# Router fed by token rows turned in the output projection, layer norm by statistics, small expert matmuls spread, last weights in pieces

## The chip, the cores and the metric

The kernel runs on one core of a Trainium2 chip. The core has a matrix engine (TensorE, PE in the profile; PEld is its weight load), a vector engine (VectorE, DVE), a scalar engine (ScalarE, ACT), GpSimd (POOL) and SyncE (SP), which issues most of the DMAs; ScalarE issues a few. Sixteen DMA engines move the data. The metric is the device time of one execution in microseconds. Three runs of the kernel before gave 2296.88, 2298.74 and 2298.82 us, median 2298.74.

## The reference, cut to what matters

Two blocks run one after the other on 256 tokens of width 1024. The change touches the second half of the second block: output projection, layer norm, router, a mixture of 32 experts (each token uses four), and a last layer norm.

```
x   = layer_norm(ALPHA * x + merged @ w_out, ln1_g, ln1_b)
logits = x @ router_w + router_b
top_val, top_idx = top_k(logits, 4);  gates = softmax(top_val)
for each expert e, on the tokens that chose it:
    gt = min(x @ w_gate[e] + b_gate[e], 7);  up = clip(x @ w_up[e] + b_up[e], -7, 7)
    y  = (gt * sigmoid(1.702 * gt) * (up + 1)) @ w_down[e] + b_down[e]
ffn = sum over the four experts of gate * y
out = layer_norm(ALPHA * x + ffn, ln2_g, ln2_b)
```

The weights w_gate, w_up and w_down are 32 x 1024 x 1024 each, in float32: 402.7 MB, all of which are read.

## The kernel before, in words

All activations of the first stages lie turned, with features on the 128 partitions: xT[:, d, 0:256] is block d (of eight) of the features, for 256 tokens. Each engine's program is one list in the order of the code; semaphores tie the lists together. The eight PSUM banks are handed out in turn by take(e, name); filled(name) is the semaphore value at which the bank has its result, emptied(name) the one at which it has been read.

Dense projections use weights in two halves. hi(t) is ScalarE's cast of weight tile t (four quarters of 128x1024), lo(t) is DVE's rest of it, and rows(...) issues the three matmuls for each of eight k. W_GATE are the gate projections, W_PA and W_PB (two tiles) the two branch projections, W_PB + 2 and W_PB + 3 the output projection w_out. The banks ("pa", d), ("pb", d) and ("wx", d) hold the results.

Behind the output projection stands the layer norm, on features that lie on partitions. TensorE adds over partitions with a matrix of 1/1024 (the mean, L810), ScalarE squares, TensorE adds again (L827), ScalarE takes the root, DVE the reciprocal, and DVE and ScalarE scale all eight blocks. TensorE multiplies with the router matrix rw (L835), turns the tokens back (L842), and turns the logits (L849). DVE finds the four largest and the positions of each token in its expert's list (the counting matmuls L854 to L856); ScalarE takes the exponentials; DVE makes G, the gate weights.

The experts are worked in 16 pairs b, with up to 64 tokens for each of the two. chosen(b) makes selection matrices Sx by comparison; gather(b) (L874) multiplies the token rows yN with them and so gathers and turns the tokens in one; XT holds the result. both(...) (L905) are the matmuls with expert weights: for each of eight k, the pair's two experts at the same time in the two halves of the columns. A pair is gate, up (each with a bias matmul, L931), the scatter of the pair before (L891, into the four banks accs), the gather of the pair after, the turn of the hidden values (L942), and down. ledger() behind pair 0 puts the expert's bias rows into accs (L963) and counts whether any expert has over 64 tokens; further pairs for such experts stand in If blocks.

The expert weights come through a ring of seven slots of 2048 KB, 12 loads for a pair, in the order gate, up, down. Load u goes into slot u % 7 and waits until TensorE has used load u - 7 (s_wused). Loads 0 to 6 take slots of the stages before as these come free.

At the end s_fin says that accs are whole. DVE adds ALPHA times the token rows, takes statistics (L1581, L1585, L1587), ScalarE the root, DVE scales and shifts (L1598, L1600), and SP stores.

## Time and profile before

| what | before |
|---|---|
| median of 3 runs | 2298.74 us |
| the profiled execution's own time | 2301.83 us |
| its span, first to last instruction | 2300.0 us |
| PE busy | 2104.4 us, 91% |
| DVE busy | 827.8 us, 36% |
| ACT busy | 575.4 us, 25% |
| DMA | 593.89 MB, mean 258 GB/s |
| mean granted TensorE clock | 0.968 |

Busy time is the time in which an engine has an instruction under way; a matmul's end is modelled, so a busy PE is not PE at its peak. The chain of waits goes back from the last instruction to what released it, and so on to the start. Its shares are PE 73%, DMA 15%, DVE 6%, ACT 3%. DMA is on the chain almost only as waiting for the experts' up weights (12% of the span).

### The profile page before, as it was taken

The numbers are of one execution on the slowest core, as the hardware profiler recorded it, in microseconds if no ns is written. First come the engines' busy times: TensorE is split into PE (matmuls) and PEld (weight loads), VectorE is DVE, ScalarE is ACT, GpSimd is POOL, SyncE is SP. The second block draws the span as 40 slices with busy tenths as digits, with TensorE's granted clock in tenths as the row PEclk, the third lists the DMA queues.
The fourth block names the chain that finished last, engine by engine and source line by source line (L and its number), as shares of the span: only waits on it lengthen the run. The fifth ranks groups of instructions, "written<-read, shape, count | busy, mean of one in ns | idle before, by whom it ended". The sixth has DMA issues, their size and how long they took to land.

```text
span 2300.0 us, 27009 instructions
## 1 busy us (share of the span) xinstructions
PE 2104.4 (91%) x11534; PEld 1402.2 (61%) x11534; DVE 827.8 (36%) x1453; ACT 575.4 (25%) x955; POOL 71.5 (3%) x119
## 2 busy tenths in 40 slices
PE   6988999999899889999998889998988999989886
PEld 3766888878687568999987843333333333333332
DVE  3353534352385656755465431111111111111113
ACT  3222423242242545544365220000000000000000
POOL 0000000000000320000041000000000000000000
PEclk7999999999999999999999989999999999999998
DMA  9543334233431564545524559999999999999994
GB/s 357 183 147 109 110 111 146 99 112 101 147 106 50 196 196 147 184 152 200 182 94 168 208 226 412 424 428 428 428 428 427 428 427 427 428 428 428 428 428 203
DMA packets 157228, 593.89 MB, mean 258 GB/s; under 512 B 6416, under 2 KB 79120, under 8 KB 132016
## 3 DMA queue, kind: packets, MB, share of 16 engines
q1 hardware_dynamic: 155104, 589.53, 64.8%
q10 hardware_dynamic: 2000, 2.57, 0.4%
q8 instruction: 94, 1.54, 0.3%
q14 instruction: 30, 0.25, 0.0%
HBM read 591.03 MB, written 1.05 MB: 257 GB/s over the span
## 4 chain that ended last, share of the span: by engine, by line
PE 73%; DMA 15%; DVE 6%; ACT 3%; issue 2%; SPq 1%; ACTq 0%; DVEq 0%
PE ps L905 21%; PE ps L278 13%; PE ps L279 13%; PE ps L280 13%; DMA ring<-in_w_up_dram 12%; PE ps L874 3%; DMA ring<-in_ada_w_dram 3%; PE ps L891 3%; DVE wr L1012 2%; PE ps L385 2%; DMA ring<-in_even_w_in_dram 1%; SPq L2044 1%; PE ps L399 1%; ACT wr L1614 1%; PE ps L942 1%
## 5 line engine op out<-in xcount | busy, mean ns | idle before, releaser
L905 PE MATMUL ps<-ring,big 128*64 128x512 f32 x3072 | 693.1, 607 | 81.9 <-DMA ring<-in_w_up_dram 51.3
L905 PEld LDWEIGHTS ps<-ring,big 128*64 128x64 f32 x3072 | 249.8, 140 | 496.3 <-issue 484.8
L278 PE MATMUL ps<-h_hi,wr 128*128 128x512 f32 (+1 forms) x960 | 342.9, 357 | 28.0 <-DVE h_lo L1064 24.9
L1012 DVE TENSOR_TENSOR wr<-ring,wr 128x1024 fp32r<-128x1024 f32 (+1 forms) x248 | 285.8, 1212 | 142.2 <-ACT wr L1614 142.1
L279 PE MATMUL ps<-h_lo,wr 128*128 128x512 f32 (+1 forms) x960 | 334.5, 348 | 0.0
L280 PE MATMUL ps<-h_hi,wr 128*128 128x512 f32 (+1 forms) x960 | 334.1, 348 | 0.0
L1614 ACT CAST wr<-ring 128x1024 fp32r<-128x1024 f32 (+1 forms) x248 | 238.7, 1032 | 128.0 <-PE ps L280 101.6
L278 PEld LDWEIGHTS ps<-h_hi,wr 128*128 128x128 f32 x960 | 186.0, 194 | 60.2 <-issue 34.5
L279 PEld LDWEIGHTS ps<-h_lo,wr 128*128 128x128 f32 x960 | 186.0, 194 | 23.8 <-issue 2.9
L280 PEld LDWEIGHTS ps<-h_hi,wr 128*128 128x128 f32 x960 | 185.6, 193 | 22.3
L1463 DVE TENSOR_SCALAR hT<-ps 128x512 f32<-128x512 f32 x32 | 20.6, 686 | 259.4 <-PE ps L931 259.4
L1476 DVE TENSOR_SCALAR hT<-ps 128x512 f32<-128x512 f32 x32 | 22.0, 688 | 239.5 <-PE ps L931 239.5
L278 PE MATMUL ps<-x_hi,wr 128*128 128x256 f32 x352 | 104.7, 297 | 1.8 <-DVE x_lo L1275 1.2
L1918 ACT COPY big<-ps 128x512 f32<-128x512 f32 x16 | 9.4, 586 | 370.9 <-PE ps L874 370.9
L279 PE MATMUL ps<-x_lo,wr 128*128 128x256 f32 x352 | 101.2, 287 | 0.0
L280 PE MATMUL ps<-x_hi,wr 128*128 128x256 f32 x352 | 101.1, 287 | 0.0
L1490 DVE COPY xT<-ps 128x512 f32<-128x512 f32 x16 | 11.1, 692 | 221.4 <-PE ps L905 221.4
L1930 ACT ACTIVATE hT<-hT 128x512 f32<-128x512 f32 x32 | 19.6, 630 | 261.2 <-DVE hT L1463 261.2
L278 PEld LDWEIGHTS ps<-x_hi,wr 128*128 128x128 f32 x352 | 69.1, 196 | 6.7 <-issue 4.4
L279 PEld LDWEIGHTS ps<-x_lo,wr 128*128 128x128 f32 x352 | 69.3, 197 | 0.2
L874 PEld LDWEIGHTS ps<-hT,big 128*128 128x128 f32 x512 | 62.3, 199 | 11.5 <-issue 11.5
L280 PEld LDWEIGHTS ps<-x_hi,wr 128*128 128x128 f32 x352 | 69.1, 196 | 0.0
(293 smaller groups left out, 2578.0 us busy)
## 6 DMA issues: line engine op xcount, KB each, us to landing
ring<-in_w_gate_dram SPq DMA_DIRECT2D x64, 2048.0 KB, 22.1
ring<-in_w_up_dram SPq DMA_DIRECT2D x64, 2048.0 KB, 19.7
ring<-in_w_down_dram SPq DMA_DIRECT2D x64, 2048.0 KB, 22.2
ring<-in_ada_w_dram SPq DMA_DIRECT2D x24, 2048.0 KB, 10.7
ring<-in_ffn_w_up_dram SPq DMA_DIRECT2D x44, 1024.0 KB, 7.6
ring<-in_ffn_w_down_dram SPq DMA_DIRECT2D x16, 1408.0 KB, 6.1
ring<-in_w_in_dram SPq DMA_DIRECT2D x9, 2048.0 KB, 8.2
ring<-in_odd_w_qkv_dram SPq DMA_DIRECT2D x6, 2048.0 KB, 8.1
```

The costliest lines, as they stand in the source:

```text
L278: e.matmul(o, l[0], r[0], start=first, stop=False)
L279: e.matmul(o, l[0], r[1], start=False, stop=False)
L280: return e.matmul(o, l[1], r[0], start=False, stop=last)
L385: ins = e.matmul(pt[32 * g:32 * g + 32, :], s2[:, 2 * g + h, :], wt[:, 2 * g + h, :], start=h == 0, stop=h == 1, skip_group_check=True)
L399: ins = e.matmul(bank(("sq", q))[:, 0:NT[q]], onesd[:, :], part[k % 2][:, 0:NT[q]], start=k == 0, stop=k == KC - 1, skip_group_check=True)
L874: ins = e.matmul(pt[:, P * c:P * c + P], yN[:, n, P * (4 * hf + c):P * (4 * hf + c) + P], Sx[turn_of(b)][:, 0, n, :], start=n == 0, stop=n ...
L891: ins = e.matmul(ps[2 * q + n][:, :], SgT[turn_of(b)][:, P * q:P * q + P], ySB[turn_of(b)][:, n, :], start=False, stop=False, skip_group_c ...
L905: ins = e.matmul(pts[hf][HALF[z], :], lhs[:, k, HALF[z]], wt[:, k % 4, 512 * hf:512 * hf + 512], start=k == 0, stop=False, skip_group_chec ...
L942: ins = e.transpose(pt[:, P * c:P * c + P], eighth(hid[:, 1, :], 4 * hf + c), ident)
L1012: e.tensor_tensor(wr[:, x], ring[:, x], h.bitcast(F32), SUB).then_inc(s_wlo, 1)
L1614: e.copy(wr[:, o], ring[:, SLOT * (t % 3) + 1024 * p:SLOT * (t % 3) + min(1024 * p + 1024, width[t])]).then_inc(s_whi, 1)
L2044: e.dma_start(view(ring, SLOT * MPLACE[m], KC, 512), a["ada_w"][m // 12].rearrange("(k p) n -> p k n", p=P)[:, :, 512 * (m % 12):512 * (m ...
```

## The change

It has five parts.

1. **Router and layer norm.** The gains and shifts of the first layer norm are no longer applied to the tokens. DVE multiplies the gain into the router matrix rw, and takes the sums that the mean and the shift need; one matmul, ("rs", 0), adds them over partitions. In the output projection, turn_rows(d) takes the place of the mean: for each block d, TensorE turns both halves of the tokens into the banks ("z", n, i), and multiplies the same blocks, as they are, with rw into ("lgt", n). DVE takes mean and variance from the z banks with bn_stats; ScalarE writes the normalised token rows yN. The gain and the shift are applied when XT is read out of PSUM, from g8b8, which 16 small DMAs on SP's queue load. DVE and ScalarE now also read XT out in four operations each.
2. **Order around it.** hi(W_PB) goes ahead of the sigmoids, the bias cast behind the last weights; lo(W_PB + 3) and the bias halves are made between the results of the output projection; the gate weights (weigh) are made behind the first four comparisons.
3. **Ledger spread.** ledger(b) does a part of the work behind each of the pairs 2, 4, 5, 6, 8, 10 and 12. In it the residual, ALPHA times yN times the gain, is also added to accs by matmuls with alphaI. The gain and the shift come as rows of 1024 words in one partition, by two DMAs on ScalarE's queue, word by word.
4. **Last weights.** The second half of up and all of down of the last pair are loaded in pieces (PIECES: load, first k, last k), with a semaphore for each; both() waits for each piece at its own k. In every pair, the second half of XT and HT is waited for at k = 4.
5. **Last norm.** last_scatter finishes tokens 0 to 127 first (s_fin 1), then the others. DVE takes statistics straight from accs, ScalarE normalises out of PSUM, DVE multiplies and adds.

```diff
+    LAST = 12 * (NE // 2 - 1)
+    PIECES = [(LAST + 6, 0, 2), (LAST + 6, 2, 3), (LAST + 6, 3, 4), (LAST + 8, 0, 2), (LAST + 8, 2, 4),
+              (LAST + 10, 0, 2), (LAST + 10, 2, 3), (LAST + 10, 3, 4)]
+    in_pieces = {u + z for u, _, _ in PIECES for z in range(2)}
...
+        pt = take(e, ("rs", 0))
+        e.wait_ge(s_rwsum, 1)
+        e.matmul(pt[:, 0:64], ones[:, :], sums, start=True, stop=True).then_inc(fullsem(("rs", 0)))
...
+        def turn_rows(d):
+            if d == 0:
+                for n in range(2):
+                    take(e, ("lgt", n), hold=True)
+            if d % 4 == 0:
+                for n in range(2):
+                    take(e, ("z", n, d // 4), hold=True)
             e.wait_ge(*emptied(("wx", d)))
+            if d == 0:
+                e.wait_ge(*emptied(("rs", 0)))
+            for n in range(2):
+                x = xT[:, d, P * n:P * n + P]
+                ins = e.transpose(bank(("z", n, d // 4))[:, P * (d % 4):P * (d % 4) + P], x, ident)
+                if d % 4 == 3:
+                    ins.then_inc(fullsem(("z", n, d // 4)))
+            for n in range(2):
+                x = xT[:, d, P * n:P * n + P]
+                ins = e.matmul(bank(("lgt", n))[:, 0:NE], x, rw[:, d, :], start=d == 0, stop=d == KC - 1,
+                               skip_group_check=True)
+                if d == KC - 1:
+                    ins.then_inc(fullsem(("lgt", n)))
...
-                    mean(d - 1)
+                    turn_rows(d - 1)
             wlast[W_PB + 2 + i] = filled(("wx", 4 * i + 3))
...
-        p2 = take(e, ("var", 0))
-        for k in range(KC):
-            e.wait_ge(s_sq, 4 * KC + k + 1)
-            e.matmul(p2[:, 0:L], onesd[:, :], part[k % 2][:, 0:L], start=k == 0,
-                     stop=k == KC - 1).then_inc(s_squsd if k < KC - 1 else fullsem(("var", 0)))
-
-
-        pt = take(e, ("lg", 0))
-        e.wait_ge(s_rw, 16)
-        for k in range(KC):
-            e.wait_ge(s_y, k + 1)
-            ins = e.matmul(pt[0:NE, 0:L], rw[:, k, :], xT[:, k, 0:L], start=k == 0, stop=k == KC - 1)
-        ins.then_inc(fullsem(("lg", 0)))
-
+        turn_rows(KC - 1)
+        for n in range(2):
...
+        def last_scatter(b):
+
+            for n in range(2):
+                e.wait_ge(*emptied(("y", b, n)))
+            for q in range(2):
+                for n in range(2):
                     ins = e.matmul(ps[2 * q + n][:, :], SgT[turn_of(b)][:, P * q:P * q + P], ySB[turn_of(b)][:, n, :], start=False,
                                    stop=False, skip_group_check=True)
-            ins.then_inc(s_scat)
-
-        def both(pts, lhs, u, first):
+                ins.then_inc(s_fin)
...
+        def both(pts, lhs, u, first, second):
 
             for k in range(KC):
+                if k == 4:
+                    e.wait_ge(*second)
                 v = u + 2 * (k // 4)
-                if k % 4 == 0:
+                if k % 4 == 0 and v not in in_pieces:
                     for z in range(2):
-                        e.wait_ge(s_w[(v + z) % 7], 16 * ((v + z) // 7 + 1))
+                        e.wait_ge(*landed_expert(v + z))
+                for i, (x, k0, _) in enumerate(PIECES):
+                    if (x, k0) == (v, k % 4):
+                        e.wait_ge(s_piece[i], 32)
...
                     e.wait_ge(*emptied(("xt", b, 0)))
-                    e.wait_ge(*emptied(("xt", b, 1)))
-                both(pts, XT[turn_of(b)], u + 4 * v, None)
+                both(pts, XT[turn_of(b)], u + 4 * v, None, emptied(("xt", b, 1)))
...
+        def ledger(b):
+
+            if b == 2:
+                pt = take(e, ("gT", 0), bank=7)
+                for n in range(2):
+                    ins = e.transpose(pt[0:NE, P * n:P * n + P], G[:, n, :], ident)
+                ins.then_inc(fullsem(("gT", 0)))
+            if b in (4, 8):
...
+            if b in (6, 10):
...
+            if b == 5:
+                e.wait_ge(*emptied(("gT", 0)))
...
+        gl, bl = (col(x, 0, 8).unsqueeze(2).to_broadcast([P, KC, NE]) for x in ("l1g", "l1b"))
+        rwb = view(part[0], 0, KC, NE)
+        e.wait_ge(s_rw, 16)
+        at = mark(e.tensor_tensor(rwb, rw, bl, MULT))
+        e.wait_ge(*at)
+        at = mark(e.tensor_tensor(rw, rw, gl, MULT))
+        mark(e.tensor_reduce(sums[:, 32:64], rwb.rearrange("p k e -> p e k"), AX, ADD))
+        e.wait_ge(*at)
+        e.tensor_reduce(sums[:, 0:32], rw.rearrange("p k e -> p e k"), AX, ADD).then_inc(s_rwsum, 1)
...
+        e.scalar_tensor_tensor(rw, bank(("rs", 0))[:, 0:32].unsqueeze(1).to_broadcast([P, KC, NE]), -1.0 / D, rw, MULT,
+                               ADD).then_inc(freesem(("rs", 0)), 1)
+
...
+            if d < 4:
+                lo(W_PB + 3, d, d + 1)
+            elif d < 6:
+                e.wait_ge(s_bhi, 1)
+                r = slice(64 * (d - 4) + NE, 64 * (d - 4) + 2 * NE)
+                e.tensor_tensor(bias_[r, :], zz[r, :], bias_[r, :].bitcast(F32), SUB).then_inc(s_blo, 1)
+            elif d == 6:
+                for n in range(2):
+                    e.wait_ge(*filled(("z", n, 0)))
+                    mark(e.bn_stats(lbst[n][:, 0, :], bank(("z", n, 0))[:, :]))
         for n in range(2):
+            e.wait_ge(*filled(("z", n, 1)))
+            at = mark(e.bn_stats(lbst[n][:, 1, :], bank(("z", n, 1))[:, :]))
+            e.wait_ge(*at)
+            at_st[n] = mark(e.bn_aggr(lmv[n], lbst[n]))
+            e.wait_ge(*at_st[n])
+            e.tensor_copy(lrt[n], lmv[n][:, 1:2]).then_inc(s_stat, 1)
+
+
+        e.wait_ge(*at_rb)
+        for n in range(2):
+            e.wait_ge(s_lroot, n + 1)
+            at = mark(e.reciprocal(lr[n], lrt[n]))
+            e.wait_ge(*at)
+            e.tensor_scalar(lnm[n], lmv[n][:, 0:1], lr[n], -1.0, MULT, MULT).then_inc(s_stat, 1)
+            e.wait_ge(*filled(("lgt", n)))
+            e.scalar_tensor_tensor(lg[:, n, :], bank(("lgt", n))[:, 0:NE], lr[n], rb, MULT, ADD).then_inc(freesem(("lgt", n)), 1)
...
+            if b == 0:
+                weigh()
...
-                freesem(("xt", b, 0)), 1)
+            for c in range(4):
+                ins = e.tensor_scalar(XT[turn_of(b)][:, c, :], bank(("xt", b, 0))[:, P * c:P * c + P], g8b8[:, c:c + 1],
+                                      g8b8[:, 8 + c:9 + c], MULT, ADD)
+            ins.then_inc(freesem(("xt", b, 0)), 1)
...
+        def spread(n):
+
+            e.wait_ge(s_troot, n + 1)
+            at = tail(e.reciprocal(sm[n][:, 1:2], sm[n][:, 0:1]))
+            e.wait_ge(*at)
+            e.wait_ge(*aggr_at[n])
+            spread_at[n] = tail(e.tensor_scalar(sm[n][:, 2:3], mv[n][:, 0:1], sm[n][:, 1:2], -1.0, MULT, MULT))
+
+        for n in range(2):
+            e.wait_ge(s_fin, n + 1)
+            for i in range(2):
+                at = tail(e.bn_stats(bst[n][:, i, :], accs[n][i][:, :]))
+                if n == 1 and i == 0:
+                    spread(0)
+            e.wait_ge(*at)
+            aggr_at[n] = tail(e.bn_aggr(mv[n], bst[n]))
...
+                e.wait_ge(s_xhat, 2 * n + i + 1)
+                at = tail(e.tensor_tensor(z, z, l2g[:, cs], MULT))
...
+                out_at[n, i] = tail(e.tensor_tensor(z, z, l2b[:, cs], ADD))
...
+
+        hi(W_PB)
         for i in range(2):
             e.wait_ge(*emptied(("gt", i, KC - 1)))
             e.activation(sg[i], sg[i], ACT.Sigmoid).then_inc(s_sig, 1)
-
-
-        hi(W_PB)
-        for i in range(4):
-            e.wait_ge(s_late[i], 16)
-        e.wait_ge(*filled(("T2", 23)))
-        e.copy(bias_[:, :], zz[:, :]).then_inc(s_bhi, 1)
         for d in range(KC):
             if d % 4 == 0:
...
+        e.activation(lst[:, 42:43], epsc[:, 0:1], ACT.Sqrt)
+        for n in range(2):
+            e.wait_ge(s_stat, n + 1)
+            e.activation(lrt[n], lrt[n], ACT.Sqrt, bias=epsc[:, 1:2]).then_inc(s_lroot, 1)
+        for n in range(2):
+            e.wait_ge(s_stat, 2 + n + 1)
+            for i in range(2):
+                e.activation(yN[:, n, :].rearrange("p (k q) -> p k q", k=KC)[:, :, 64 * i:64 * i + 64],
+                             bank(("z", n, i))[:, :].rearrange("p (q k) -> p k q", k=KC), ACT.Identity, bias=lnm[n],
+                             scale=lr[n]).then_inc(freesem(("z", n, i)), 1)
+
+
+        e.dma_start(bdn[0:NE, :], a["b_down_2"]).then_inc(s_late2[0], 16)
+        e.wait_ge(s_blo, 2)
+        flat = a["cols"].rearrange("p c -> c p")
+        for row, sem_, c in ((grow, s_rowg, COLS["l1g"]), (bdn[NE:NE + 1, :], s_rowb, COLS["l1b"])):
+            e.dma_start(row.rearrange("o (c p) -> o c p", c=KC), flat[c:c + KC, :].unsqueeze(0),
+                        allow_slow_non_contiguous=True).then_inc(sem_, 16)
         e.dma_start(l2g, a["ln2_2"][0:1, :].to_broadcast([P, D])).then_inc(s_late2[1], 16)
         e.dma_start(l2b, a["ln2_2"][1:2, :].to_broadcast([P, D])).then_inc(s_late2[2], 16)
-        for n in range(2):
-            for i in range(2):
...
+            e.wait_ge(*spread_at[n])
+            for i in range(2):
+                e.activation(zN[:, n, 512 * i:512 * i + 512], accs[n][i][:, :], ACT.Identity, bias=sm[n][:, 2:3],
+                             scale=sm[n][:, 1:2]).then_inc(s_xhat, 1)
...
+            if u in in_pieces and z == 1:
+                for i, (x, k0, k1) in enumerate(PIECES):
+                    for y in range(2 * (x == u - 1)):
+                        e.dma_start(view(ring, SLOT * XS[(x + y) % 7], SLOT)[:, D * k0:D * k1], src[
+                            2 * (u // 12) + y].rearrange("(p k) n -> p (k n)", k=KC)[
+                            :, SLOT * hf + D * k0:SLOT * hf + D * k1]).then_inc(s_piece[i], 16)
...
+        for i, x in enumerate(("l1g", "l1b")):
+            src = a["cols"].rearrange("(b k) c -> c b k", k=KC)
+            for c in range(KC):
+                e.dma_start(g8b8[16 * c:16 * c + 16, 8 * i:8 * i + 8], src[COLS[x] + c],
+                            allow_slow_non_contiguous=True).then_inc(s_g8, 16)
```

The instructions around the layer norm on TensorE. ps are the PSUM banks, konst the unit matrix or the triangle, part the squares, big in L835 and L849 the router matrix, hT the selection. Before, behind the last blocks of the output projection:

```order
L810 MATMUL ps<-xT,onesd 128x256 [waits s_bank_free0]
L827 MATMUL ps<-part,onesd 128x256 [waits s_square,s_bank_free1]
L827 MATMUL ps<-part,onesd 128x256 [waits s_square] x7
L835 MATMUL ps<-xT,big 32x256 [waits s_ln_out,s_rw,s_bank_free2]
L835 MATMUL ps<-xT,big 32x256 [waits s_ln_out] x7
L842 MATMUL ps<-konst,xT 128x128 [waits s_bank_free3]
L842 MATMUL ps<-konst,xT 128x128 x3
L842 MATMUL ps<-konst,xT 128x128 [waits s_bank_free4]
L842 MATMUL ps<-konst,xT 128x128 x3
L849 MATMUL ps<-konst,big 128x32 [waits s_bank_free2,s_bank_free5]
L849 MATMUL ps<-konst,big 128x32
```

And the changed kernel, from the last matmul of block 7 to the first gather (L892):

```order
L285 MATMUL ps<-x_hi,wr 128x256
L844 MATMUL ps<-konst,xT 128x128 [waits s_bank_free0]
L844 MATMUL ps<-konst,xT 128x128
L849 MATMUL ps<-big,xT 128x32 x2
L844 MATMUL ps<-konst,xT 128x128 [waits s_bank_free1]
L844 MATMUL ps<-konst,xT 128x128
L849 MATMUL ps<-big,xT 128x32 x2
L872 MATMUL ps<-big,konst 128x32 [waits s_router,s_bank_free2]
L873 MATMUL ps<-big,ones 128x32
L874 MATMUL ps<-big,konst 128x32
L892 MATMUL ps<-hT,big 128x128 [waits s_bank_free6,s_bank_free5,s_bank_free4,s_bank_free7,s_chosen]
```

The variance, the router matmuls on turned data and the turning of tokens and logits have gone from between the projection and the counting matmuls; the transposes and router matmuls stand between the blocks.

ScalarE's list from the yN writes (L1988) to the first read of XT (L2012), in the changed kernel; big is yN, the bias rows, and the exponentials in turn:

```order
L1988 ACTIVATE big<-ps,part 128x8x64 [waits s_ln_stats]
L1988 ACTIVATE big<-ps,part 128x8x64
L1993 DMA big<-in_b_down_dram 32x1024
L1997 DMA zz<-in_cols_dram 1x1024x1 [waits s_bias_lo]
L1997 DMA big<-in_cols_dram 1x1024x1
L1999 DMA big<-in_ln_2_dram 128x1024
L2000 DMA big<-in_ln_2_dram 128x1024
L2003 ACT_TABLE_LOAD
L2003 ACTIVATE big<-big 128x4 [waits s_router_neg]
L2003 ACTIVATE big<-big 128x4
L2012 ACTIVATE big<-ps,xT 128x128 [waits s_bank_full7,s_gain_cols]
```

Five DMA issues stand between the token rows and the exponentials, two of them of single words.

## Rows read from the trace of the kernel before

**Rows 1.** The page's slices: GB/s moved in each fortieth of the span.
```profile
GB/s 357 183 147 109 110 111 146 99 112 101 147 106 50 196 196 147 184 152 200 182 94 168 208 226 412 424 428 428 428 428 427 428 427 427 428 428 428 428 428 203
```

**Rows 2.** Chain of waits from 1200 us: start us, us, what.
```profile
1347.73 13.95 PE ps L905 x64
...
2232.62 20.16 DMA ring<-in_w_up_dram
...
2266.17 13.95 PE ps L905 x64
```

**Rows 3.** Windows: us, busy by engine, granted clock, DMA share, GB/s.
```profile
1334.00:1355.00 21.00, 14.89 (x74) 10.32 (x76) 4.88 (x19) 5.51 (x10) 0.00 (x0) 0.76 0.00 1
...
1354.00:1358.00 4.00, 4.00 (x20) 1.55 (x18) 0.00 (x0) 0.00 (x0) 0.00 (x0) 1.00 0.58 197
...
1415.00:1420.00 5.00, 5.00 (x26) 1.84 (x24) 0.00 (x0) 0.00 (x0) 0.00 (x0) 1.00 0.73 259
...
1500.00:2200.00 700.00, 629.22 (x2904) 264.30 (x2904) 102.01 (x223) 38.66 (x72) 3.25 (x11) 0.98 1.01 428
```

**Rows 4.** Timeline around W_PB: start us, us, instruction [idle before it, releaser].
```profile
1245.78 1.28 ACT L1870 ACT_TABLE_LOAD   x1
1247.08 3.71 ACT L1870 ACTIVATE big<-big 128x2048 f32<-128x2048 f32 x2
1250.69 3.87 ACT L1614 CAST wr<-ring 128x1024 fp32r<-128x1024 f32 x4
...
1251.75 4.63 DVE L1012 TENSOR_TENSOR wr<-ring,wr 128x1024 fp32r<-128x1024 f32 x4 [5.53 <-ACT wr L1614]
1256.30 2.73 DVE L1353 TENSOR_TENSOR big<-big,ps 128x256 f32<-128x256 f32 x8
...
1256.82 0.55 PE L278 MATMUL ps<-ob_hi,wr 128*128 128x256 f32 x1 [5.98 <-DVE wr L1012]
```

**Rows 5.** Timeline in the output projection, DVE and PE.
```profile
1289.37 2.47 DVE L1370 TENSOR_TENSOR bias<-zz,bias 32x1024 fp32r<-32x1024 f32 x2
...
1292.34 1.22 PE L810 MATMUL ps<-xT,onesd 128*128 128x256 f32 x2 [4.54 <-DVE xT L1374]
```

**Rows 6.** Window behind that wait.
```profile
1292.30:1296.00 3.70, 3.66 (x15) 3.48 (x16) 0.32 (x1) 0.00 (x0) 0.00 (x0) 0.50 0.02 4
```

**Rows 7.** Groups of 1316 to 1341 us: form, count | busy us, mean ns | idle before.
```profile
L1908 ACT COPY big<-ps 128x512 f32<-128x512 f32 x4 | 3.7, 1071 | 2.3 <-PE ps L842 2.3
...
L842 PE MATMUL ps<-konst,xT 128*128 128x128 f32 x16 | 2.2, 280 | 0.0
```

**Rows 8.** Timeline of the router and the first gather.
```profile
1332.67 0.29 DVE L1400 MAX8 big<-big 128x8 f32<-128x32 f32 x2
...
1335.01 0.38 PE L854 MATMUL ps<-big,konst 128*128 128x32 f32 x2 [1.61 <-DVE big L1415]
...
1340.17 6.57 PE L874 MATMUL ps<-hT,big 128*128 128x128 f32 x32 [4.34 <-issue]
```

**Rows 9.** DMA queues of 1066 to 1076 us: packets, MB, share of 16 engines.
```profile
q1 hardware_dynamic: 1040, 2.10, 59.0%
q10 hardware_dynamic: 1040, 0.13, 8.4%
```

**Rows 10.** Timeline of SP's queue, an issue of an expert load.
```profile
1251.35 2.65 SPq L2104 DMA_DIRECT2D ring<-in_w_gate_dram  x1
```

**Rows 11.** Timeline of the last pair and the tail.
```profile
2243.13 8.78 PE L905 MATMUL ps<-ring,big 128*64 128x512 f32 x32 [2.44 <-DMA ring<-in_w_up_dram]
...
2280.39 3.67 PE L891 MATMUL ps<-xT,big 128*128 128x512 f32 x8 [0.27 <-issue]
...
2284.22 1.02 DVE L1581 SCALAR_TENSOR_TENSOR big<-big,ps 128x512 f32<-128x512 f32 x1 [4.23 <-PE ps L994]
2285.27 0.69 DVE L1585 BATCH_NORM_STATS2 wk<-big 128x6 f32<-128x512 f32 x1
...
2296.76 0.75 DVE L1600 SCALAR_TENSOR_TENSOR big<-big,sm 128x512 f32<-128x512 f32 x1
```

More of the change, by code:

```diff
@@ L992, in pe @@
                 scatter(b)
-        scatter(NE // 2 - 1)
-        e.matmul(ps[7][0:1, 0:1], ones[:, 0:1], ones[:, 0:1], start=True, stop=True,
-                 skip_group_check=True).then_inc(s_fin)
+        e.wait_ge(*emptied(("sgt", NE // 2 - 1)))
+        last_scatter(NE // 2 - 1)
     def dve(e):
@@ L1530, in dve @@
             expert_out(b)
-            if b == 0:
-                ledger()
+            ledger(b)
         e.wait_ge(s_ovi, 2)
```

303 lines of the change are left out of this document (142 added, 161 removed).

## The prediction

> **What bounds the kernel now.** I read the page's slices of the span first. From the 25th of 40 on, the core moves 424 to 428 GB/s in every slice but the last [rows 1]: the expert stage, 192 loads of 2048 KB, is bound by its transfers. The chain of waits from 1200 us on says what happens at its two ends. The first expert matmuls start at 1347.73 us, and the first two pairs of experts are a chain of TensorE work. From the third pair to the last, the chain passes through about 20 us of waiting for up weights in each pair, and it ends in the down matmuls of the last pair at 2266.17 [rows 2].
>
> The windows show why the start matters as much as the rate. The ring holds seven loads. They land while the router is still at work, and then the transfers stand idle: share 0.00 from 1334 to 1355 us. They start again within 1354 to 1358, when TensorE has used the first quarter of pair 0 and frees two slots. Later they are full (share 1.01, 428 GB/s over 1500 to 2200), but for one hole at 1415 to 1420 (share 0.73) [rows 3]. So the restart at about 1355 plus a fixed stream plus a tail is the whole time. Every microsecond taken out ahead of the first expert matmul comes out of the end; one taken out inside a middle pair does not, since TensorE waits there anyway.
>
> **The change, part by part**, in the time of the profiled execution (span 2300.0, its own time 2301.83).
>
> *Router sums* (new, behind the value projection): one small TensorE matmul, and six DVE operations. DVE is idle there, so four of them are done before TensorE comes; the matmul and the two that read it lie on the path to the first scores. About +0.3; from 0 to +1.5.
>
> *The cast of W_PB ahead of the sigmoids.* Before, ScalarE loads a table and takes both sigmoids (1245.78 to 1250.7), casts W_PB until 1254.5, DVE makes the low halves until 1256.3, and TensorE stands 5.98 us [rows 4]. Now the cast begins at 1245.8, and the low halves end at about 1251.5. But all eight banks hold ("pa", d), and DVE frees the first only behind the first sigmoid: 1245.8 + 3.9 + 1.3 + 1.9 = 1252.9. TensorE starts at 1253.6 instead of 1256.82: -3.2, where removing the wait would have given -5. It is still a gap of about 2.7 us, so I count the slow first microseconds as before. DVE's later steps there keep their distances, so the output projection starts 3.2 earlier too. Bounds: -2 to -5.
>
> *The output projection.* Before, DVE makes the low halves of W_PB + 3 and the bias rows (2.47 us) before it empties the first result; TensorE stands 4.54 us [rows 5] and then runs at a granted clock of 0.50, which is 1.2 GHz [rows 6]. From the end of the second column block to the end of the mean matmuls are 28.4 us (1287.8 to 1316.2). Now DVE alternates: result, quarter of the weights. A block is 2.88 us of matmuls (24 at 0.12). Each turn_rows is two transposes, at 0.14 each (16 rows of L842 in 2.2 us are two to a record and overlap) and two router matmuls at 0.21 each (the distance of L854's start to the next matmul's) [rows 7, 8]: 0.7 us. The fourth quarter of the low halves is made only behind result 3, and block 4 waits for it: 0.45 + 1.15 - 0.7, about 1.0 us. So 8 x 0.7 + 6 x 2.88 + 1.0 = 23.9 us, at the full clock, since nothing stands long: -4.5. Bounds: -2.5 to -5.5.
>
> *Layer norm, router, selection.* Before, from 1316.2 to the first gather at 1340.17 are 24.0 us: squares, variance, root, reciprocal, scaling, router, two turns, top four, then the exponentials and gate weights, and the gather behind all of these [rows 8]. Now, from the last turn_rows: statistics of two banks and their aggregation 2.3 (0.69 each, rows 11), eight small steps for root, shift, logits and maximum 1.6, from MAX8 to the position matmuls 2.2 (2.34 before, with two maxima), these and the four comparisons 2.3. The gate weights are made behind the comparisons. That is 8.0 instead of 24.0: -16.0. What runs beside it: ScalarE writes yN in four operations of 0.92 [rows 7], ready about 2 us before the gather. Bounds: -13 to -17.
>
> *Gather to first expert matmul.* Before 7.56 us, the gather's 6.57 at the low clock. Now the gather again at the low clock, then the gate turn: 6.95, as the second half of XT is asked for only at k = 4. -0.6. ScalarE's queue has about 1 us to spare here: five DMA issues, a table load, the exponentials (4.2 us together), then 2.5 us on DVE for gate weights and four comparisons, then the copy.
>
> *The gain and shift loads.* 16 loads of 16x8 single words on SP's queue stand ahead of an expert load and of W_PB + 3's raw tile, and two of 1024 single words on ScalarE's ahead of the exponentials. No row shows single-word loads. The nearest is the router's load, 1040 packets of 128 bytes: 8.4% of 16 engines over 10 us, 13 ns a packet; packets of 2 KB beside it cost 59% for 1040, 91 ns [rows 9]. And an issue can block: the third expert load took 2.65 us where others take 0.4, with some three loads outstanding [rows 10]. If the words are spread, a row load is 128 packets on each of eight engines, 1.7 to 11.6 us; the second issue waits for most of the first. I take the small end, 0.5 us an issue, since the nearest row in size is the 13 ns one; the large end costs 12 us. SP's 16 issues (about 8 us) fit into its wait for the next tile. Cost 0; bounds 0 to +12.
> The Trainium skill (DMA: Bandwidth & Descriptors, Rules for kernel authors) says that a strided last dimension becomes one descriptor for each element, and asks to rearrange it; that speaks against these loads. By it and the 13 ns row the two row loads are 2048 descriptors, 3.3 us on eight engines, of which about half would hold ScalarE; no run here shows it yet.
>
> *The ledger spread over pairs.* Before it stood behind pair 0 and left the hole at 1415 to 1420: 0.27 x 5 us, and some 0.15 around it. Now each piece lies where TensorE waits for up weights for some 20 us. -1.5; bounds 0 to -2. The pieces in pairs 4 to 12 add up to 3 us behind a pair, all under that wait.
>
> Together the first expert matmul comes 0.3 - 3.2 - 4.5 - 16.0 - 0.6 = 24.0 us earlier (about 1323.7), and the stream 25.5.
>
> *Last pair.* The first up half waits for its load and runs slow (8.78 for 32 matmuls, [rows 11]), until 2251.9; the second half then waits 1.0 for its load. In pieces it goes on at once: -1.0 (-2.7 if the clock does not fall). HT's second half asked for later: -0.5. The down matmuls then end 1.5 earlier; their last load has landed by 2272, before they reach it.
> The same page (Bandwidth) says to batch transfers to 1 MiB for 75% of the peak and gives 2.0 us plus bytes over rate for one. By it ten more transfers cost up to 20 us. In this trace queued loads do not pay a start each: 2048 KB loads run at 428 GB/s, 4.9 us each, without the 2 us.
>
> *Tail.* Before, the scatter's 3.67 us, a marker matmul, DVE from 2284.22 to 2297.51 [rows 11]. Now the scatter starts 0.5 later (both copies waited for), but rows 0 to 127 are whole after half of it, so the statistics start at 2282.9 in the old timing. Four of them at 0.69, two aggregations and the small steps end at about 2286.8, against 2291.4; ScalarE's four normalisations run beside. Four pairs of 0.69 operations and one interruption follow: 6.0. End 2292.8 instead of 2297.5: -4.7; bounds -3.5 to -5.5.
>
> Sum: -24.0 - 1.5 - 1.5 - 4.7 = -31.7. The profiled execution would be 2270.1. It stood 3.1 above the median of 2298.74, so the predicted time is 2267.
>
> **Rivals.**
> A. The word loads hold the queues. For it: no row shows them, and rows 10 show that an issue can block. Against: the spare microsecond and the 13 ns. If each row load costs 91 ns a packet, ScalarE is late by 6 to 12: 2273 to 2279.
> B. The pieces slow the end of the stream. For it: sixteen transfers where six were; against: they are queued ahead, like all others. If each small one costs 1 us: 2277 to 2283.
> C. The clock stays at 2.4 GHz through the shorter gaps (before W_PB, at the gather). Then -1.9, and up to -3 if DVE is in time: 2262 to 2265.
> D. The stream does not restart earlier, as if something other than the freed slots held it. Then only last pair and tail remain: 2292. Against it: the restart comes a quarter of a pair (7 us) behind the first expert matmul, at share 0.00 before.
> E. Slower. A row load of one partition may run on one engine. Then 2048 packets stand in one queue behind each other on ScalarE's path to the exponentials: 26 us at 13 ns, 186 at 91. It takes over from 16 ns a packet, where the wait passes the 31.7 won: 2300 and more. Against: what the load writes is cut into eight rows of 128.
> By the same page's rule on the number of engines (why a DMA increments its semaphore by 16), the slowest dimension, eight here, sets it: eight engines, not one. No row of before has such a load.
>
> **How the numbers follow.** Forecast 0.62, A 0.15, B 0.05, C 0.10, D 0.03, E 0.05. The forecast's own terms give 2261 to 2272; with C, A and most of B the range is 2259 to 2281. A measurement of this kernel tells 0.2%, 4.6 us, from no change. Faster by more than that is all but E and a remnant for what I have not thought of: 0.93; the same 0.02; slower 0.05.
>
> **What would show it.** Right: W_PB's first matmul about 2.7 us after W_PA's last; no stop at block 0's result and one of 1 us before block 4; the gather about 8 us behind the last turn_rows; the first expert matmul at 1322 to 1326; the transfers' idle stretch about 12 us instead of 21, and no hole behind pair 0; DVE's tail near 10 us. Wrong: ScalarE's exponentials more than 3 us behind its yN writes (A, E); less than 428 GB/s in the last pair (B); a restart of the transfers that does not follow the first quarter of pair 0 (D).

## The result and the profile after

| what | before | after |
|---|---|---|
| median | 2298.78 us | 2272.9 us (four runs, 2270.95 to 2274.9) |
| ratio to before, 95% interval | | 0.9887 [0.987, 0.9904] |
| span of the profiled execution | 2300.0 us | 2272.1 us |
| mean granted TensorE clock | 0.968 | 0.973 |

The change makes the kernel 25.9 us faster; 31.7 were forecast. The time lies inside the range of 2259 to 2281, between the forecast's own terms, which ended at 2272, and rival A, which began at 2273. The traces say which of the two it was. The two profiled executions differ by 27.9 us, 2.0 more than the medians; the sums by stage below are for them.

The page's slices of the changed kernel, GB/s moved, answer to [rows 1]: the stream is full from the 25th slice. Before, the 25th had 412 and the 26th 424 (the prediction read 424 to 428 from the 25th on).

```profile
GB/s 361 186 149 111 111 111 148 100 114 102 148 80 77 186 178 145 186 165 179 194 115 87 270 267 428 428 427 427 428 428 427 428 428 426 429 428 427 428 428 272
```

The timeline of the changed kernel around W_PB and in the output projection (start us, us, engine and instruction, idle time before it with what ended it) answers to [rows 4, 5].

```profile
1244.23 3.90 ACT L1712 CAST wr<-ring 128x1024 fp32r<-128x1024 f32 x4
1248.15 1.28 ACT L1970 ACT_TABLE_LOAD   x1
1249.45 3.71 ACT L1970 ACTIVATE big<-big 128x2048 f32<-128x2048 f32 x2
1251.39 2.74 DVE L1424 TENSOR_TENSOR big<-big,ps 128x256 f32<-128x256 f32 x8 [1.43 <-ACT big L1970]
1251.91 0.36 PE L283 MATMUL ps<-ob_hi,wr 128*128 128x256 f32 x1 [2.49 <-issue]
1291.43 0.39 PE L283 MATMUL ps<-x_hi,wr 128*128 128x256 f32 x1 [1.07 <-DVE wr L1067]
```

DVE's first product waits for the first sigmoid, and TensorE starts 0.5 us behind it: the bank was the second wait, as said. The 4.54 us stop at block 0 has gone, and one of 1.07 us stands before block 4.

From the norm to the first pair, the same view, first on TensorE, then on ScalarE's queue and DVE (the first line is the last turned row, which ends at 1306.51; an engine name with q is its DMA issues):

```profile
1305.98 0.53 PE L849 MATMUL ps<-big,xT 128*128 128x32 f32 x4
1311.70 0.61 PE L872 MATMUL ps<-big,konst 128*128 128x32 f32 x2 [5.18 <-DVE big L1485]
1314.60 6.62 PE L892 MATMUL ps<-hT,big 128*128 128x128 f32 x32 [1.45 <-issue]
1328.64 0.69 PE L900 MATMUL ps<-konst,hT 128*128 128x128 f32 x2 [7.41 <-DVE big L1533]
1329.26 3.68 PE L940 MATMUL ps<-ring,big 128*64 128x512 f32 x8
```
```profile
1309.32 0.32 ACTq L1993 DMA_DIRECT2D big<-in_b_down_dram  x1
1309.69 1.28 ACTq L1997 DMA_DIRECT2D zz<-in_cols_dram  x1
1310.99 7.43 ACTq L1997 DMA_DIRECT2D big<-in_cols_dram  x1
1318.47 3.80 ACTq L1999 DMA_DIRECT2D big<-in_ln_dram  x1
1322.30 0.45 ACTq L2000 DMA_DIRECT2D big<-in_ln_dram  x1
1322.78 1.28 ACT L2003 ACT_TABLE_LOAD   x1 [11.38 <-issue]
...
1324.78 0.17 DVE L1498 RECIPROCAL big<-big 128x2 f32<-128x2 f32 x1 [10.27 <-ACT big L2003]
```

The first gather starts 8.09 us behind the last turned row (1306.51); 8.0 was forecast. Then the second load of single words holds ScalarE's queue for 7.43 us and the load behind it for 3.80. ScalarE, done with the token rows at 1311.4, reaches the exponentials' table at 1322.78. DVE stands 10.27 us for the exponentials and TensorE 7.41 for DVE. That is rival A's mechanism, and the prediction's own sign of it: the exponentials stand more than 3 us behind the token rows.

The windows of the changed kernel (us, busy by engine, granted clock, DMA share, GB/s) answer to [rows 3]:

```profile
1329.00:1331.00 2.00, 2.00 (x6) 0.54 (x6) 0.09 (x1) 1.62 (x2) 0.00 (x0) 0.50 0.00 0
1331.00:1333.00 2.00, 2.00 (x8) 0.71 (x6) 0.00 (x0) 0.04 (x1) 0.00 (x0) 0.50 0.00 0
...
1338.00:1345.00 7.00, 7.00 (x34) 2.24 (x32) 0.00 (x0) 0.00 (x0) 0.00 (x0) 1.00 0.78 297
...
1500.00:2200.00 700.00, 639.37 (x2946) 273.83 (x2944) 118.76 (x281) 47.98 (x106) 3.23 (x11) 0.98 1.01 428
```

The stall has a second price. Behind it TensorE begins pair 0 at a granted clock of 0.50. SP's issue of the eighth load, which waits for the first slot, gets it at 1339.12, 9.9 us behind the first expert matmul; before it was 7.4 (1355.13 less 1347.73).

```profile
1290.20 48.92 SPq L2204 DMA_DIRECT2D ring<-in_w_up_dram  x4
```

The last pair and the tail, answering to [rows 11]:

```profile
2223.67 13.95 PE L940 MATMUL ps<-ring,big 128*64 128x512 f32 x64 [2.05 <-DMA ring<-in_w_up_dram]
...
2243.34 13.95 PE L940 MATMUL ps<-ring,big 128*64 128x512 f32 x64 [0.54 <-DVE big L1564]
...
2258.11 3.67 PE L921 MATMUL ps<-xT,big 128*128 128x512 f32 x8 [0.81 <-ACT xT L2034]
```
```profile
2260.53 1.30 DVE L1683 BATCH_NORM_STATS2 wk<-ps 128x6 f32<-128x512 f32 x2 [3.37 <-PE ps L921]
...
2268.95 0.69 DVE L1698 TENSOR_TENSOR big<-big 128x512 f32<-128x512 f32 x1
```

All 64 up matmuls go without a stop and at the full clock, and DVE's last operation ends 12.35 us behind the last down matmul (2257.29), where it was 17.39.

### The profile page after: what moved, and what is told of

The parts are those of the page before. It is cut to its first block, busy times and chain, and to the rows that moved or that the text cites. A ratio compares the mean times of both kernels' runs of the same rounds, so it can differ in the third digit from the quotient of the medians.

```text
span 2272.1 us, 27092 instructions
## 1 busy us (share of the span) xinstructions
PE 2092.2 (92%) x11528; PEld 1397.2 (61%) x11528; DVE 837.5 (37%) x1507; ACT 583.3 (26%) x993; POOL 71.8 (3%) x119
## 4 chain that ended last, share of the span: by engine, by line
PE 74%; DMA 16%; DVE 5%; ACT 3%; issue 1%; ACTq 1%; SPq 1%; DVEq 0%
PE ps L940 21%; PE ps L283 14%; PE ps L284 13%; PE ps L285 13%; DMA ring<-in_w_up_dram 12%; DMA ring<-in_ada_w_dram 3%; PE ps L911 2%; PE ps L892 2%; DVE wr L1067 2%; PE ps L405 2%; ACT big L2012 1%; PE ps L419 1%; PE ps L413 1%; PE ps L720 1%; PE ps L965 0%
## 5 line engine op out<-in xcount | busy, mean ns | idle before, releaser
L2012 ACT ACTIVATE big<-ps,xT 128x128 f32<-128x128 f32 x64 | 24.1, 456 | 361.7 <-PE ps L892 361.7
L284 PE MATMUL ps<-f_lo,wr 128*128 128x512 f32 x176 | 68.6, 390 | 0.0
```

The lines of the kernel that those rows point to most:

```text
L284: e.matmul(o, l[0], r[1], start=False, stop=False)
L2012: ins = e.activation(XT[turn_of(b)][:, 4 + c, :], bank(("xt", b, 1))[:, P * c:P * c + P], ACT.Identity, bias=g8b8[:, 12 + c:13 + c], scale ...
```

## The experiments

Ratios are to the kernel before on the same chip, with the 95% interval; 0.001 is 2.3 us. Differences are taken between ratios, since the runs came in several sets. Each ratio is uncertain by 0.001 to 0.003. Of the kernels below, whole rows, early rows and the last two fill runs have intervals apart from the changed kernel's. For the others the trace carries the argument, with one execution each.

**Where the issues stand.** The first kernel moves the five DMA issues on ScalarE's queue.

```diff
-        e.dma_start(bdn[0:NE, :], ...)      # and the four behind it
         e.wait_ge(s_gneg, 1)
...
         gathered(0)
         gates_turned(0)
+        e.dma_start(bdn[0:NE, :], ...)      # and the four behind it
```

> The changed kernel with ScalarE's five DMA issues (expert bias rows, the two rows of single words, the two rows of the last norm) moved behind its first read of XT and the turned gate weights; nothing else. In the changed kernel's trace these issues take from 1309.32 to 1322.75 us, the exponentials follow, DVE stands 10.27 us for them, TensorE 7.41, and then pair 0 begins at the low clock until about 1334. Theory (the issues hold ScalarE): the first expert matmul comes 7 us earlier against the block before it, at about 7.4 us behind the start of the first gather instead of 14.7; it runs at the full clock, so the transfers restart about 10 us earlier; 2263 us, about 0.984 of before. Rival 1 (the exponentials are late for another reason, such as the table load or DVE): nothing changes, 2273. Rival 2 (the transfers cannot restart earlier, since loads 5 and 6 land only at 1318 and the rest of the stream is bound by something else): the first expert matmul moves, the end does not, 2271 to 2273.

Measured: 2268.63 us, 0.9864 [0.9847, 0.988]: 5.3 us less than the changed kernel, not 10, and the intervals just overlap. The wait for the issues did go. The first expert matmul starts at 1319.48, 13.4 us behind the last turned row instead of 22.8, at the full clock, and the slot is free at 1326.92. But the stream does not start then; the windows of this kernel:

```profile
1320.00:1325.00 5.00, 5.00 (x26) 1.69 (x24) 0.00 (x0) 1.33 (x5) 0.00 (x0) 1.00 0.66 46
1325.00:1330.00 5.00, 5.00 (x26) 1.72 (x24) 0.00 (x0) 1.15 (x1) 0.00 (x0) 1.00 1.27 55
1330.00:1335.00 5.00, 5.00 (x25) 1.56 (x22) 1.10 (x2) 0.37 (x1) 0.00 (x0) 1.00 0.91 268
```

The queue of the expert loads in 1330 to 1335 (packets, MB, share of 16 engines):

```profile
q1 hardware_dynamic: 39, 0.64, 30.1%
```

The DMA engines are busy (share 0.66 and 1.27) while they move 46 and 55 GB/s: the words, and then the last norm's rows, keep engines from the expert weights. The 0.64 MB are 1.5 us of a full stream, so it counts as full from about 1333.5, 6.6 us after the slot was free. The length agrees: from the freed slot to the last pair's first up matmul are 890.7 us here, and 884.3 with whole rows (the next experiment). So both the theory and rival 2 were half right: moving the words late trades a wait of ScalarE for one of the stream. How much of it is the words' and how much the norm's rows' is not told apart; in the kernel before, these rows and the bias rows, 1.18 MB, moved in about 4.5 us.

**The words themselves.**

```diff
-            e.dma_start(row.rearrange("o (c p) -> o c p", c=KC), flat[c:c + KC, :].unsqueeze(0), ...)
+            e.dma_start(row, a["ln2_2"][0:1, :])
```

> The changed kernel with the two rows loaded from a place where 1024 words lie together, at the same place in ScalarE's queue (so gain and shift of the residual are wrong values; the amount of data is the same). Theory (single words): an issue takes 0.3 to 0.5 us as the ones beside it did, ScalarE reaches the exponentials about 2 us behind its last write of yN, and the kernel gains like the one with the issues moved, 2263 to 2265 us. Rival (the issues wait because loads 5 and 6 of the experts keep the DMA engines busy until 1318): the issue of the second row or of the next load still takes 5 us or more, and the time stays at 2270 to 2273.

Measured: 2263.6 us, 0.9846 [0.9829, 0.9862]. The kernel loads the last norm's gain in place of both rows, so only its time counts. ScalarE's issues in it:

```profile
1309.55 0.53 ACTq L1997 DMA_DIRECT2D zz<-in_ln_dram  x1
...
1310.11 0.23 ACTq L1997 DMA_DIRECT2D big<-in_ln_dram  x1
1310.37 0.36 ACTq L1998 DMA_DIRECT2D big<-in_ln_dram  x1
```

The same bytes, issued into the same busy engines (share 0.90 to 1.01 until 1320), take 0.53 and 0.23 us instead of 1.28 and 7.43. So it takes the many packets to hold the queue; load on the engines from others alone doesn't. The two rows of words cost 9.4 us in all (0.0041). The queue of ScalarE's loads in the changed kernel in 1318 to 1322 (packets, MB, share of 16 engines) gives an estimate of the price of one:

```profile
q10 hardware_dynamic: 1610, 0.01, 54.9%
```

0.549 x 16 x 4 us over 1610 packets is 22 ns a packet, nearer to the 13 ns that I took than to the 91. The share is about what eight busy engines would give (0.50), and the row is cut into eight parts. This is weak evidence: single microseconds of the stretch read 0.23 to 1.28. The Trainium skill (DMA: Bandwidth & Descriptors, Why a DMA increments its semaphore by 16 and not by 1) lets the slowest dimension set the number of engines, which makes eight of them; the share does not speak against it. The same page of the Trainium skill (Rules for kernel authors) turns a strided last dimension into one descriptor for each element. The trace agrees: the 1610 packets carry 0.01 MB, about four bytes each.

**Earlier instead of later.** ScalarE waits from 1285 to 1307, and the DMA engines are idle from about 1302.

```diff
         e.activation(lst[:, 42:43], epsc[:, 0:1], ACT.Sqrt)
+        e.dma_start(bdn[0:NE, :], ...)      # and the four behind it
         for n in range(2):
             e.wait_ge(s_stat, n + 1)
```

> The changed kernel with the same five DMA issues moved ahead of the layer norm's roots on ScalarE's queue, where it waits for DVE from 1285 to 1307 us (they may start at about 1300, when the bias halves are done); nothing else. Moving them behind the first pair's start won 5.3 us of the 9.4 that whole rows won: the words then ran on eight DMA engines while the expert transfers tried to restart (48 GB/s where 428 are usual, 1320 to 1330). Theory (two prices: ScalarE's hold and the engines' time): at 1300 to 1307 ScalarE and the DMA engines are both idle, so both go, and the time is that of the whole rows, 2263.5 us, ratio 0.985. Rival 1 (only ScalarE's hold counts, the rest was chance): 2268, as with the issues moved back. Rival 2 (the second row and the last norm's rows are held 8 us and now keep ScalarE from the roots, on the path): 2270 or more.

Measured: 2263.84 us, 0.9843 [0.983, 0.9857]. These are the words at the price of whole rows. The second issue takes 0.69 us here and not 7.43, with the same number of packets and hardly a transfer beside them; that a full queue has to drain first fits both, and is an inference. The engines' time is not saved but falls where it is not missed:

```profile
1305.00:1310.00 5.00, 0.22 (x2) 0.11 (x1) 4.58 (x23) 3.27 (x6) 0.00 (x0) 0.90 0.59 53
...
1320.00:1325.00 5.00, 5.00 (x26) 1.76 (x26) 0.00 (x0) 3.05 (x6) 0.00 (x0) 1.00 0.32 134
```

Until 1310 the words and the norm's rows hold up the expert loads behind them (53 GB/s). But these loads still land, at about 1323, before the first slot is free at 1327.54.

**The cast of W_PB.** The two sigmoids ahead of it again.

```diff
-        hi(W_PB)
         for i in range(2):
             e.wait_ge(*emptied(("gt", i, KC - 1)))
             e.activation(sg[i], sg[i], ACT.Sigmoid).then_inc(s_sig, 1)
+        hi(W_PB)
```

> The changed kernel with the two sigmoids ahead of the cast of W_PB again, as before; nothing else. Theory: TensorE stands 6 us instead of 2.49 before the first W_PB matmul, everything behind it comes 3.5 us later, 2276.4 us. Rival (the exponentials wait for DMA issues that end at their own time, so a later start is absorbed there): 2273.

Measured: 2276.48 us, 0.99 [0.9882, 0.9918], 3.0 us by the ratios, whose intervals overlap. In the trace the wait before W_PB is 5.98 us again, and the gather's start 3.6 us later against W_PA's. The rival has a share: TensorE's wait behind the gather is 6.44 us, not 7.41, and the first slot comes free 8.6 us behind the first expert matmul, not 9.9. Against W_PA it is only 1.3 us later. Beside the stall of the words the new order is worth less than its 3.5 us.

**The ledger behind one pair.**

```diff
-            ledger(p)
+            for x in (2, 4, 5, 6, 8, 10, 12) if p == 1 else ():
+                ledger(x)
```

> The changed kernel with all seven pieces of the ledger behind pair 1 and not behind pairs 2 to 12. Theory (a piece costs nothing only where TensorE waits for weights): behind pair 1 TensorE sets when slots come free, the transfers get a hole like that of before (which was 2.0 us of bytes at 1415 to 1420), larger since the residual is in it: +2 to +5, 2275 to 2278. Rival (the place is indifferent, since the chain gives TensorE 10 to 20 us of waiting later in any case): 2273.

Measured: 2280.12 us, 0.9914 [0.99, 0.9927]: 6.2 us by the ratios, more than the 2 to 5 that I had allowed. Two of the waits in it, and the windows behind:

```profile
1448.79 2.07 PE L997 MATMUL ps<-zz,ones 1*128 1x512 f32 x2 [0.26 <-DVE big L1588]
1453.00 3.51 PE L1004 MATMUL ps<-xT,alphaI 128*128 128x512 f32 x4 [2.13 <-DVE xT L1583]
```
```profile
1450.00:1460.00 10.00, 7.06 (x22) 2.60 (x22) 3.21 (x10) 0.00 (x0) 0.00 (x0) 0.69 0.70 297
1460.00:1465.00 5.00, 5.00 (x26) 1.67 (x24) 0.00 (x0) 0.00 (x0) 0.00 (x0) 1.00 0.00 0
1465.00:1470.00 5.00, 5.00 (x26) 1.63 (x24) 0.00 (x0) 0.00 (x0) 0.00 (x0) 1.00 0.82 308
```

TensorE is in the ledger from 1437.65 to 1457.99, 20.3 us, part of it at the low clock, and the transfers lose 9.5 us of bytes: (1 - 297/428) x 10 + 5 + (1 - 308/428) x 5. From the first freed slot to the last pair's first up matmul are 894.0 us, against 884.6 in the changed kernel. Spread over seven pairs, the same instructions leave the transfers at 428.

**Whole last weights.**

```diff
-    PIECES = [(LAST + 6, 0, 2), (LAST + 6, 2, 3), ...]
+    PIECES = []
```

> The changed kernel with the last pair's second up half and its down weights loaded whole, as before. Theory (a piece lets TensorE go on while the rest lands): TensorE stops at k = 4 of the last up and waits for 1 to 3 us, +1.0 to +3.4, 2274 to 2276. Rival (in the changed kernel the last weights land well before TensorE reaches them anyway): 2273.

Measured: 2276.47 us, 0.9905 [0.989, 0.9921], 4.1 us by the ratios, again with overlapping intervals. The trace shows it in detail:

```profile
2222.47 8.78 PE L939 MATMUL ps<-ring,big 128*64 128x512 f32 x32 [2.02 <-DMA ring<-in_w_up_dram]
2232.27 7.09 PE L939 MATMUL ps<-ring,big 128*64 128x512 f32 x32 [1.01 <-DMA ring<-in_w_up_dram]
```

From the first up matmul to the first down matmul are 22.56 us instead of 19.67: 1.0 of waiting and 1.7 of low clock. But the low clock lies in the first half (8.78 against 7.09), which is loaded whole in both kernels and lies ahead of the stop. Other kernels that have the pieces settle it. The same matmuls with issues late:

```profile
2217.65 15.65 PE L940 MATMUL ps<-ring,big 128*64 128x512 f32 x64 [2.06 <-DMA ring<-in_w_up_dram]
```

Behind a wait of 2.04 to 2.08 us these 64 take 15.65 us in four kernels with pieces (issues late, old casts, and the runs without fillers and with twelve below), and 13.95 behind 2.05 in the changed kernel. So the 1.7 us are not the pieces' doing; with one execution of each, they look like chance. Where the clock fell too, first up to first down are 21.4 us, and the pieces are worth 1.2.

**Filling TensorE's wait.** On the early rows, the last quarter of the low halves behind result 2, and ten matmuls without a use:

```diff
-            if d < 4:
-                lo(W_PB + 3, d, d + 1)
+            if d < 3:
+                lo(W_PB + 3, d, d + 1 + d // 2)
...
         pt = take(e, ("pos", 0))
+        for _ in range(10):
+            e.matmul(pt[:, 256:512], ones[:, :], konst[:, 0:256], start=True, stop=True)
         e.wait_ge(s_gate, 2)
```

> The kernel with the early rows, and two things more: the last quarter of the low halves of W_PB + 3 is made behind result 2 of the output projection with the third, and ten matmuls of 128x256 without a use are issued on TensorE while it waits for the positions. Theory: the wait of 1.06 us before block 4 goes; TensorE no longer stands 5.2 us, so the first gather's 32 matmuls take 3.6 us as they do in later pairs and not 6.6; the first expert matmul comes 4 us earlier than with early rows alone, and the end too: 2259.5, ratio 0.983. Rival 1 (DVE's and ScalarE's reading of the gathered rows and the gate weights decide, not the gather): -1.5, 2262. Rival 2 (the clock falls all the same, or the filling matmuls run into the position matmuls): no gain from them, 2262.5.

Measured: 2261.9 us, 0.986 [0.9834, 0.9886], with two of the five times at 2273 to 2274; no gain that can be told from early rows. The trace shows why:

```profile
1304.68 7.61 PE L872 MATMUL ps<-konst,ones 128*128 128x256 f32 x20 [2.28 <-DVE big L1470]
```

take() waits for a bank, and the one whose turn it was is emptied only by DVE's logits. TensorE stood 2.28 us, the clock fell, and ten fillers took 7.61 us instead of fitting into 5.2. The position matmuls came 4.6 us later than without them, the faster gather gave 2.8 of that back, and the first expert matmul stands 16.0 us behind the last turned row, where early rows alone have 14.9. Two more runs: without the ten fillers, and with twelve in a bank that is taken earlier.

> The kernel with the early rows and the last quarter of the low halves made behind result 2; no filling matmuls. The version with fillers reached 2261.9 (ratio 0.986) against 2263.8 (0.9843) of early rows alone: its fillers began only 2.28 us behind the last turned rows, ran at 0.76 each at the low clock and pushed the position matmuls back. Theory (that cost 1.1 us, the earlier quarter gives 1.06): 2262.8 here, and the stop before block 4 gone. Rival (the quarter costs as much as it gives, since DVE is late for a result): 2263.8, with a stop elsewhere.

Measured: 2262.86 us, 0.9843 [0.9829, 0.9857]. The stop before block 4 is gone in the trace; its 1 us is below what the times can tell.

```diff
         turn_rows(KC - 1)
+        pt = take(e, ("pos", 0))
+        for _ in range(12):
+            e.matmul(pt[:, 256:512], ones[:, :], konst[:, 0:256], start=True, stop=True)
         for n in range(2):
             held.discard(full["lgt", n][0])
...
-        pt = take(e, ("pos", 0))
         e.wait_ge(s_gate, 2)
```

> The same with twelve filling matmuls of 128x256, now in a bank that is taken ahead of the release of the eight held ones, so that they can start right behind the last turned rows. Theory (the low clock in the gather comes from TensorE standing for 5.2 us ahead of it): the fillers take about 0.38 each and end before DVE's counts are ready, the three position matmuls and the gather run at the full clock, 3.0 to 3.5 us less than without them, 2259.5, ratio 0.983. Rival 1 (the clock falls all the same in the two short waits that remain): gather 6.6 us, no gain. Rival 2 (ScalarE's and DVE's reading of XT decides): the gather is faster, the first expert matmul comes less than 1 us earlier.

Measured: 2259.18 us, 0.9827 [0.9813, 0.9841]. The fillers and the gather in the trace, and without fillers the gather alone:

```profile
1305.85 5.43 PE L866 MATMUL ps<-konst,ones 128*128 128x256 f32 x24
```
```profile
1312.80 5.99 PE L892 MATMUL ps<-hT,big 128*128 128x128 f32 x32 [1.45 <-issue]
```

With fillers right behind the last turned rows the clock is 1.00 from 1300 to 1320, the gather takes 3.81 us, and the first expert matmul comes 11.5 us behind the last turned row instead of 14.2. The end follows, 3.7 us; all four times (up to 2261.1) lie below all four without fillers (from 2262.25). This version beats both kernels, the changed one by 0.0060 (13.8 us) with intervals that do not overlap, and before by 0.0173 (39.8 us).

**What varies ahead of the change.**

> The kernel before, unchanged, in another profiled execution. In the first one W_PA's first matmul started at 1244.92 us, in the changed kernel's at 1243.50, although nothing ahead of it moved to account for it. Theory (it varies from one execution to the next): another start here, anywhere in 1242.5 to 1245, and the same distances behind it: 5.98 us before W_PB, 102.8 us from W_PA's first matmul to the first expert matmul, 17.4 us from the last down matmul to DVE's last. Rival (the change gains 1.4 us in an earlier stage): 1244.9 again.

Measured: one time, 2300.01 us, span 2298.2. W_PA starts at 1241.62, below the 1242.5 to 1245 that I had put. The wait before W_PB is 5.98 us, the first expert matmul comes at 1344.52 (102.9 us behind W_PA's first), and DVE ends 17.2 us behind the down matmuls. Ten executions of the changed kernel and its variants, alike up to there, have W_PA's first matmul between 1240.66 and 1244.26. So the 1.4 us by which the changed kernel's profile was early can be chance, and nothing speaks for another cause.

## Why the prediction was right in sign and where it failed in size

Term by term, from the two profiles (after less before):

| term | forecast | measured |
|---|---|---|
| ahead of W_PA (router sums) | +0.3 | -1.4, within the spread |
| cast of W_PB first | -3.2 | -3.5 |
| output projection | -4.5 | -4.6 (28.4 to 23.8) |
| norm, router, selection | -16.0 | -15.9 (23.9 to 8.1) |
| gather to first expert matmul | -0.6 | +7.1 (7.56 to 14.66) |
| first matmul to restart of transfers | 0 | +2.5 |
| stream to the last pair's up weights | -1.5 | -3.4 |
| last pair | -1.5 | -3.4 (23.04 to 19.67), 1.7 of it the clock |
| last down matmul to the end | -4.7 | -5.1 |

With the W_PB products themselves, 0.2 us shorter, these make the 27.9 between the spans.

The three large terms on the path held to 0.3 us: they were built from durations of the nearest rows and from the question what waits second. In one the parts do not add up to the 8.0 that was written: 2.3, 1.6, 2.2 and 2.3 are 8.4, and 8.09 was measured. W_PB shows the use of that question: the wait that was removed was 5.98, the gain 3.5, since the bank came next.

**That the profiles differ from the forecast by only 3.8 us (27.9 against 31.7) is in part luck.** The stall costs 10.2 us against the forecast sum (7.7 before the first expert matmul, 2.5 behind it). Everything else gives 6.4 back, and 3.4 of that are the early W_PA and the clock in the last pair, which another execution need not have.

**The step that failed** is the gain and shift loads: "I take the small end, 0.5 us an issue ... Cost 0". The price of a packet was of the right size, by the estimate of 22 ns. What I left out was the queue. I asked how long a load's packets take, and not what an issue waits for when the packets before it, 1024 for the row and then 1024 more, stand behind expert loads. ScalarE then had one microsecond to spare and needed eleven. The prediction did price this case, as rival A, at 6 to 12 us, and it measures 9.4, though at 22 ns a packet and not at A's 91; it had 0.15 and deserved the first place. The issue of 2.65 us among three outstanding loads [rows 10] was the row that said so. I also overlooked that a stall ahead of the first pair costs the clock: 2.5 us, since pair 0 started at 0.50; where the words do not stand there, pair 0 frees its slot after 7.4 us again.

Rival E did not come about: 1610 packets passed in 4 us, where E's single engine would take 21 us at its 13 ns. Rival C did not either: the clock fell at W_PB (0.56) and in the gather (0.50). Nor did D: the restart follows the first free slot. The sixteen word loads on SP's queue took 14.8 us of issues where I had put 8, and nothing waited for them.

**Last pair**: I priced the piece at -1.0, "-2.7 if the clock does not fall", and took the first. Both held. The changed kernel's execution kept the clock, and 3.4 came out with HT's half microsecond; four executions of its variants did not, and there 23.04 becomes 21.4, 1.7 less where 1.5 was forecast. The pieces did not decide which of the two it was. Rival B did not come about: the share stays at 1.00 to 1.02 in the last pair, and the pieces land in time.

**Ledger**: of the 3.4 us, 2.0 is the hole of 1415 to 1420 by bytes (259 GB/s where 428 is usual); by its DMA share, which I had used, it was 1.4. The slice before it (418 GB/s over 1400 to 1415) holds 0.35. About 1 us stays open. From the first freed slot to the last pair's first up matmul, the kernel before takes 888.0 and 889.7 us in its two profiles, and eight kernels with the ledger spread and no transfers in the way 884.2 to 884.6. So the gain is real, and its size lies between 3.4 and 5.5.

The tail was not tried apart. That it is 5 us rests on the two traces alone.

## What to carry to other kernels

Count the packets of a small DMA, not its bytes, and ask what stands behind its issue on the same engine: 8 KB in 2048 words cost 9.4 us where ScalarE was needed next and expert loads ran, and nothing that could be measured at a place where ScalarE waited and the loads behind had time to spare. Moving such a load later is not the same as moving it away; look at which transfer it meets there. Where TensorE's clock drops in a short wait just ahead of the critical stretch, work without a use can pay, if nothing, a bank's release included, delays its start. And before a difference of one profile is put down to the change, look at the same place in the profiles of its variants: 1.7 us of the last pair went away there.

## What the runs showed of the hardware that I had not expected

- An issue of a load of 1024 words took 1.28 us as the first one. As the second it took 7.43 in the changed kernel, 1.77 in the run with ten fillers, 0.74 with issues late and 0.69 with issues early, depending on what the queue and the engines still had to do.
- While such words run, and the norm's rows behind them, the DMA share reads 0.66 to 1.27 at 46 to 55 GB/s: a full share says nothing of bandwidth.
- A wait of 1.07 us left the clock at 1.00; those of 2.28, 2.49 and 5.2 us were followed by 0.50 to 0.56. With fillers in the 5.2 us, the gap of 1.45 us behind them left it at 1.00.
- Much the same wait can end either way. Ahead of the last pair's up matmuls, 2.02 to 2.08 us were followed by the low clock in five kernels, but 2.05 in the changed one and 2.21 with the ledger behind pair 1 by the full one. Waits of 1.35 to 1.46 us there left it at 1.00 in three kernels.
